# Key pages of a paged attention laid across partitions in quarters, queries block-diagonal

## The reference

```
x = x + 1/2 * SwiGLU_1(RMSNorm(x))
z = RMSNorm(x) @ w_in         # pooling u, attention q k v (6 heads x 64), retention q k v g
x = x + concat(pooling, attention, retention) @ w_out
x = x + 1/2 * SwiGLU_2(RMSNorm(x))
```

```
gate[block] = mean over the block's keys of q.k     # 4 past blocks of 256 keys
3 of the 4 past blocks are kept, the one with the lowest gate is dropped
s[key] = q.k / 8 - slope[h] * (position of q - position of key)
p = softmax(s over kept past keys and own keys up to j);   out = p @ v
```

## Time and profile before

| | |
|---|---|
| median of 3 runs | 1308.75 us |
| the profiled execution | 1308.36 us, span 1306.7 us, 1.66 us around it |
| TensorE, matmul | busy 1296.9 us (99%), 10969 instructions |
| TensorE, weight loads | 1253.0 us (96%) |
| DVE | 764.6 us (59%) |
| ACT | 650.2 us (50%) |
| GpSimd | 232.7 us (18%) |
| granted TensorE clock, mean | 0.998 |
| DMA | 233.18 MB, mean 178 GB/s |

### The profile page before, as it was taken

How to read it: one execution, slowest core, us unless ns; L and a number is a source line. 1 busy time by engine, 2 the same in 40 slices (tenths; PEclk the granted TensorE clock), 3 DMA queues, 4 the chain that set the end, 5 groups by cost and what they waited for, 6 DMA issues and landing times.

```text
span 1306.7 us, 27046 instructions
## 1 busy us (share of the span) xinstructions
PE 1296.9 (99%) x10969; PEld 1253.0 (96%) x10969; DVE 764.6 (59%) x787; ACT 650.2 (50%) x734; POOL 232.7 (18%) x372
## 2 busy tenths in 40 slices
PE   9999999999999999999999999999999999999998
PEld 7999999999879999999999999999998799999998
DVE  5555555677676655644555555565866675555433
ACT  6555543435463655553365555333446456555433
POOL 1020000357541000000101000012865220000010
PEclk9999999999999999999999999999999999999999
DMA  6665444658895444444445554446589844444442
GB/s 196 201 211 185 161 139 151 208 177 227 262 350 170 133 161 145 144 153 145 153 156 183 183 174 132 149 149 215 168 254 321 284 129 161 160 133 157 145 149 68
DMA packets 211423, 233.18 MB, mean 178 GB/s; under 512 B 14974, under 2 KB 205192, under 8 KB 211348
## 3 DMA queue, kind: packets, MB, share of 16 engines
q1 hardware_dynamic: 203388, 209.10, 50.1%
q0 software_dynamic: 7840, 23.01, 5.3%
q10 hardware_dynamic: 120, 0.03, 0.0%
HBM read 226.90 MB, written 5.32 MB: 178 GB/s over the span
## 4 chain that ended last, share of the span: by engine, by line
PE 96%; DMA 1%; DVE 1%; SPq 1%; issue 0%; ACT 0%; ACTq 0%; DVEq 0%
PE ps L1427 24%; PE ps L1429 24%; PE ps L1428 24%; PE ps L1547 4%; PE ps L1549 4%; PE ps L1548 4%; PE ps L1698 2%; PE ps L1736 2%; DMA kbuf<-in_cache_k 1%; PE ps L1875 1%; PE ps L1877 1%; PE ps L1876 1%; PE ps L1716 1%; PE ps L1588 1%; SPq L403 0%; DMA g_rows<-in_pool_scale 0%
## 5 line engine op out<-in xcount | busy, mean ns | idle before, releaser
L695 ACT ACTIVATE w_hi<-w_raw 128x2048 fp32r<-128x2048 f32 x167 | 319.8, 1915 | 521.6 <-PE ps L1429 418.5
L1007 DVE TENSOR_TENSOR w_lo<-w_raw,w_hi 128x2048 fp32r<-128x2048 f32 x159 | 366.1, 2303 | 194.4 <-ACT w_hi L695 190.0
L1427 PE MATMUL ps<-h_hi,w_hi 128*128 128x320 f32 x768 | 237.9, 310 | 0.7 <-DVE h_lo L1093 0.7
L1429 PE MATMUL ps<-h_hi,w_lo 128*128 128x320 f32 x768 | 237.3, 309 | 0.0
L1428 PE MATMUL ps<-h_lo,w_hi 128*128 128x320 f32 x768 | 237.3, 309 | 0.0
L1427 PE MATMUL ps<-g_hi,w_hi 128*128 128x320 f32 x704 | 218.0, 310 | 0.0
L1429 PE MATMUL ps<-g_hi,w_lo 128*128 128x320 f32 x704 | 217.5, 309 | 0.0
L1428 PE MATMUL ps<-g_lo,w_hi 128*128 128x320 f32 x704 | 217.5, 309 | 0.0
L1427 PE MATMUL ps<-act_hi,w_hi 128*128 128x320 f32 x704 | 216.5, 308 | 0.0
L1428 PE MATMUL ps<-act_lo,w_hi 128*128 128x320 f32 x704 | 216.5, 308 | 0.0
L1429 PE MATMUL ps<-act_hi,w_lo 128*128 128x320 f32 x704 | 216.5, 308 | 0.0
(11 more groups left out here) (295 smaller groups left out, 1734.0 us busy)
## 6 DMA issues: line engine op xcount, KB each, us to landing
w_raw<-in_ffn_w_in SPq DMA_DIRECT2D x87, 1024.0 KB, 5.1
w_raw<-in_ffn_w_out SPq DMA_DIRECT2D x32, 896.0 KB, 4.8
w_raw<-in_w_in SPq DMA_DIRECT2D x22, 1024.0 KB, 5.5
kbuf<-in_cache_k SPq DMA_DIRECT2D x96, 192.0 KB, 3.2
w_raw<-in_ffn_w_out SPq DMA_DIRECT2D x16, 1024.0 KB, 5.2
w_raw<-in_w_out SPq DMA_DIRECT2D x8, 1024.0 KB, 7.1
kbuf<-in_cache_k POOLq DMA_DIRECT2D x32, 192.0 KB, 3.0
kbuf<-in_cache_v SPq DMA_DIRECT2D x32, 192.0 KB, 4.3
```

Of the source, the lines that this page charges most:

```text
L695: act.activation(w_hi[:, slot, :], w_raw[:, slot, :], ACT.Copy).then_inc(hi_done, 1)
L1007: dve.tensor_tensor(w_lo[:, slot, :], w_raw[:, slot, :], w_hi[:, slot, :].bitcast(F32), ALU.subtract).then_inc(split_done, 1)
L1427: pe.matmul(out, w_hi[:, slot, w], hi[:, k, :], start=(k == 0), stop=False)
L1429: ins = pe.matmul(out, w_lo[:, slot, w], hi[:, k, :], start=False, stop=(k == k_all - 1))
```

## The change

The key pages of a sequence are loaded four side by side: page 4*half + j goes to partitions 32j to 32j+31, four consecutive tokens (6144 bytes) on one partition. After the same DVE transposes, partitions 32a to 32a+31 hold the dimensions of page a of a group of four. The queries are laid block-diagonally: on partitions 32a to 32a+31 only columns 8a to 8a+7 are filled. A product then uses all 128 rows and 32 columns; output row (sequence, head half g, page a, query), and the three heads of g lie side by side in columns: 768 past scores and 3 x 32 own scores a row, in banks 2 and 3. A row no longer holds all keys of a query, so that block sums, maxima and sums of exponentials are brought together by 32x32 transposes on DVE. Copies that reorder the transposed probabilities are more and smaller, and the three addr_align calls go away (the table is empty).

```
-                        sp_e.dma_start(kbuf[home][:, 4 * half + j, :],
-                                       A["cache_k"][L, page[j]].rearrange("t h d -> t (h d)")).then_inc(k_landed[home][half], 16)
+                        sp_e.dma_start(kbuf[home][32 * j:32 * j + 32, 4 * half:4 * half + 4, :],
+                                       A["cache_k"][L, page[j]].rearrange("(t r) h d -> t r (h d)", r=4)).then_inc(k_landed[home][half], 16)
```

```
 def qprep(L, p):
-                for bb in range(2):
-                    for gg in range(2):
-                        ...
-                        ins = pool.tensor_copy(dst.rearrange("p s (j c) -> p s j c", j=2)[:, :, :, 0:8],
-                                               q_rep[:, 3 * gg:3 * gg + 3, :, p * 16 + 8 * bb:p * 16 + 8 * bb + 8])
+                for a in range(4):
+                    r = slice(32 * a, 32 * a + 32)
+                    for bb in range(2):
+                        dst = q_sc[p][r, 384 * bb:384 * bb + 384].rearrange("p (x c) -> p x c", c=32)[:, :, 8 * a:8 * a + 8]
+                        src = q_rep[r, :, :, p * 16 + 8 * bb:p * 16 + 8 * bb + 8].rearrange("p h j q -> p (h j) q")
+                        ins = pool.tensor_copy(dst, src)
...
```

```
 def exps(p, parts=range(9)):
+                        n, part = divmod(k, 3)
+                        a, b = (256 * n + P * part, 256 * n + P * part + P) if part < 2 else (768 + 32 * n, 800 + 32 * n)
+                        at_b = 32 * part + n
+                        ins = act.activation(sp[p][:, a:b], sp[p][:, a:b], ACT.Exp, bias=bias_s[:, at_b:at_b + 1],
+                                             accum_out=blk[:, at_b:at_b + 1])
 def probs_evac(p):
+                    for n in range(3):
+                        ...
+                        for quad in range(2):
+                            at = 256 * (n % 2) + P * quad
+                            past = ps[:, t_bank(p, n // 2), at:at + P].rearrange("p (g a q) -> p g a q", g=4, a=4)
+                            to = pt[:, 384 * quad:384 * quad + 384].rearrange("p (a g n q) -> p g a n q", a=4, g=4, n=3)[:, :, :, n, :]
+                            ins = act.activation(to, past, ACT.Copy)
+                        ...
+                    for bb in range(2):
+                        ...
+                        act.activation(to, own, ACT.Copy)
-                exps(3, (0, 1))
+                exps(3, range(4))
                 out_evac(0)
                 act.wait_ge(stored_va, 16 * (L + 1))
                 att_evac(2)
-                exps(3, (2, 3, 4))
+                exps(3, range(4, 9))
```

```
 def soft_in(p):
+                    raw = ps[:, 2:4, :].rearrange("p b n -> p (b n)")
+                    dve.tensor_reduce(past_blocks(0), raw[:, 0:768].rearrange("p (n k x) -> p n k x", n=3, k=2), AX, ALU.add)
+                    dve.tensor_tensor(sp[p][:, 0:768].rearrange("p (k t r) -> p k r t", k=6, r=4), raw[:, 0:768]..., cst["alibi_s"][:]..., ALU.add)
+                    dve.tensor_tensor(sp[p][:, 768:864], raw[:, 768:864], cst["alibi_own"][:, p, :], ALU.add).then_inc(sm_in, 1)
+                    dve.drain()
+                    dve.tensor_reduce(past_blocks(2), sp[p][:, 0:768].rearrange("p (n k x) -> p n k x", n=3, k=2), AX, ALU.max)
+                    dve.tensor_reduce(blk[:, 128:131], sp[p][:, 768:864].rearrange("p (n x) -> p n x", n=3), AX, ALU.max)
 def soft_bias(p):      # a drain stands between steps that depend on each other
+                    dve.transpose(blk[:], blk[:])                          # 128 x 160
+                    dve.tensor_tensor(w, sums..., sums..., ALU.add)        # 128 x 32
+                    dve.tensor_tensor(peak..., peaks..., peaks..., ALU.max)
+                    dve.tensor_reduce(peak[:, 4, :], blk[:, 128:160]..., AX, ALU.max)
+                    dve.tensor_reduce(least, w..., AX, ALU.min)
+                    dve.tensor_tensor(w, w, each(least, 4), ALU.is_le)
+                    dve.tensor_tensor(w, w, cst["rank"]..., ALU.mult)
+                    dve.tensor_reduce(last, w..., AX, ALU.max)
+                    dve.tensor_tensor(w, w, each(last, 4), ALU.is_equal)
+                    dve.scalar_tensor_tensor(out=peak..., in0=w, scalar=-BIG, in1=peak..., op0=ALU.mult, op1=ALU.add)
+                    dve.tensor_reduce(top, peak..., AX, ALU.max)
+                    for e in range(2): dve.scalar_tensor_tensor(out=bias_s..., in0=w, scalar=-BIG, in1=each(top, 4), ...)
+                    dve.tensor_scalar(bias_s[:, 64:96]..., each(top, 4), -1.0, None, ALU.mult)
+                    dve.transpose(bias_s[:], bias_s[:]).then_inc(sm_bias, 1)   # 128 x 96
 def soft_sum(p):       # transpose 96, reduce, multiply by own_head, transpose 32, reduce, reciprocal: 6 for 2
```

```
-                FETCH = {2: 99, 5: 0, 10: 244}
+                FETCH = {}
+                def key_scores(p):
+                    pe.wait_ge(kt_ok, L * 16 + p * 4 + 4)
+                    for n in range(3):
+                        for j in range(2):
+                            for g in range(4):
+                                c = (3 * (g % 2) + n) * HD + 32 * j
+                                at_q = 192 * g + 64 * n + 32 * j
+                                ins = pe.matmul(ps[32 * g:32 * g + 32, 2 + n // 2, 256 * (n % 2):256 * (n % 2) + 256],
+                                                q_sc[p][:, at_q:at_q + 32], kbuf[k_home(p, g // 2)][:, :, c:c + 32],
+                                                start=(j == 0), stop=(j == 1))
```

More of the change, by code:

```diff
@@ L545, in qprep @@
                     r = slice(HD * half, HD * half + HD)
-                    own = q_bd[r, 0:192].rearrange("p (b x) -> p b x", b=2)
-                    for f in range(3):
-                        ins = pool.tensor_copy(own[:, :, 8 * half + 40 * f:8 * half + 40 * f + 8],
-                                               q_smp[r, f, p * 16:p * 16 + 16].rearrange("p (b q) -> p b q", b=2))
+                    own = q_bd[r, :].rearrange("p (f x) -> p f x", f=3)[:, :, 40 * half:40 * half + 40]
+                    for bb in range(2):
+                        ins = pool.tensor_copy(own[:, :, 32 * bb:32 * bb + 8],
+                                               q_smp[r, :, p * 16 + 8 * bb:p * 16 + 8 * bb + 8])
                 ins.then_inc(qb_ok, 1)
@@ L845, in ret_square, with exps @@
                     act.activation(o_sq[:, f, :], ps[:, 6, 0:TOK], ACT.Square).then_inc(o_sqd, 1)
[L847 removed]
+                def exps(p, parts=range(9)):
                     if 0 in parts:
                         act.wait_ge(sm_bias, L * 4 + p + 1)
[L850 to L854 removed]
+                    for k in parts:
+                        n, part = divmod(k, 3)
[3 more added lines that the diff above has]
+                                             accum_out=blk[:, at_b:at_b + 1])
+                    if 8 in parts:
                         ins.then_inc(sm_exp, 1)
@@ L1215, in soft_bias @@
                     dve.drain()
-                    dve.tensor_scalar(ss[:, 32:37], ss[:, 20:25], ss[:, 30:31], None, ALU.subtract).then_inc(sm_bias, 1)
+                    dve.tensor_reduce(last, w.rearrange("p c q -> p q c"), AX, ALU.max)
+                    dve.drain()
+                    dve.tensor_tensor(w, w, each(last, 4), ALU.is_equal)
+                    dve.drain()
+                    dve.scalar_tensor_tensor(out=peak[:, 0:4, :], in0=w, scalar=-BIG, in1=peak[:, 0:4, :], op0=ALU.mult, op1=ALU.add)
@@ new lines, in soft_bias @@
+                    dve.drain()
+                    dve.tensor_reduce(top, peak.rearrange("p c q -> p q c"), AX, ALU.max)
+                    dve.drain()
+                    for e in range(2):
+                        dve.scalar_tensor_tensor(out=bias_s[:, 0:64].rearrange("p (c e q) -> p c e q", e=2, q=NT)[:, :, e, :],
+                                                 in0=w, scalar=-BIG, in1=each(top, 4), op0=ALU.mult, op1=ALU.subtract)
+                    dve.tensor_scalar(bias_s[:, 64:96].rearrange("p (a q) -> p a q", q=NT), each(top, 4), -1.0, None, ALU.mult)
@@ new lines, in soft_sum @@
+                    dve.drain()
+                    dve.tensor_tensor(ss[:, 0:32].rearrange("p (n q) -> p n q", q=NT), ss[:, 32:40].unsqueeze(1).to_broadcast([P, 4, NT]),
+                                      cst["own_head"][:].unsqueeze(2).to_broadcast([P, 4, NT]), ALU.mult)
+                    dve.drain()
+                    dve.transpose(ss[:, 0:32], ss[:, 0:32])
+                    dve.drain()
+                    dve.tensor_reduce(ss[:, 96:97], ss[:, 0:3], AX, ALU.add)
+                    dve.drain()
@@ L1714, in transpose_probs @@
                         pe.wait_ge(pt2_evac, L * 8 + p * 2)
-                    for j in range(8):
+                    for j in range(6):
                         ins = pe.transpose(ps[:, t_bank(p, j // 4), P * (j % 4):P * (j % 4) + P], sp[p][:, P * j:P * j + P], ident[:])
@@ L1718, in transpose_probs @@
                             ins.then_inc(pt2_done, 1)
```

(6 more changed lines are left out.)

138 lines of the change are left out of this document (67 added, 71 removed).

## The result

| | before | after |
|---|---|---|
| median of the runs | 1308.88 us (1308.27 to 1309.34) | 1320.05 us (1318.97 to 1325.3) |
| ratio of the times, 95% interval | | 1.0094 (1.0067 to 1.0121) |
| profiled execution, span | 1308.36, 1306.7 us | 1318.97, 1317.1 us |

The change makes the kernel 0.94% slower. Forecast was 1312.0 with a range of 1300 to 1319: slower is right, the size is not, and the time lies 1 us outside the range.

The account below looks back on a forecast made before the run. The prediction took TensorE, busy 99% of the span, as the bound. A layer's terms, -5.0 + 2.6 + 1.8 + 0.3 + 2.0 + 0.1 = +1.8, twice +3.6, on 1308.4 gave 1312.0 us; range 1300 to 1319.

Parts of the forecast that it names:

- the clock: A clock under 1.00 behind the new waits was named only as a sign; the sum leaves it out.
- TensorE's products: key_scores in 2.62 us for 3.95, a gain of 1.33; with own_scores -1.24 a pair, -5.0 us a layer.
- DVE's string: On DVE before evac_last of the same chunk: soft_in -0.65 and soft_bias +2.0, together +1.35 us.
- Wait 1: Scores of pair 1: TensorE comes earlier, DVE's maxima later, so it stands +2.6 us, bounds 0.5 and 3.6.
- Wait 2: Scores of pairs 2 and 3: key pages written to 32 partitions land later, +1.8 us a layer.
- Rival B: At pairs 2 and 3 the key pages land in time, the sum without 1.8: 1308.4 us; chance 0.22.
- rival D: Half-rate key pages decide at pairs 2 and 3, +11.6 us in all: 1320.0 us; chance 0.11.
- Wait 3: Chunk boundaries around soft_bias(1) to (3), evac_last waiting behind DVE's longer string: +0.3 us a layer, 0 to 1.5.
- Wait 4: Pooling products L1842, fed by a longer chain from chunk 11's end to vr_tokens: +2.0 us a layer, 0 to 3.
- Instruction offsets: The three offset calls only shift TensorE's instruction stream: 0, bounds -1 and +2.5 us in all.
- C: TensorE's gain survives, decided on DVE between soft_in(0) and smax(1): 1298.5 to 1303.5 us; chance 0.20.

Follow-up runs that it names:

- e4_scores_only: Kernel before with only key_scores changed, to 24 products of 128 rows: 1300.19 us, ratio 0.9936.
- e6_scores_bias: Kernel before with key_scores changed to 24 products and soft_bias longer by 9 dependent DVE operations, key loads as before: 1315.87 us.
- f3_short_bias: Changed kernel without six dependent steps of soft_bias, so that no block is dropped: 1310.23 us, ratio 1.0019.
- e1_no_smax: Changed kernel without TensorE's three waits for the prompt's maxima before the scores of pairs 1, 2 and 3: 1321.08 us.
- e3_filler: Changed kernel with 21 extra TensorE products in front of the wait for the maxima at pair 1: 1322.50 us.
- e7_quarter_loads: Kernel before with each key page loaded onto 32 partitions, four tokens in a row: 1312.84 us, ratio 1.0032.
- e2_old_loads: Changed kernel with each key page loaded over all 128 partitions, as before: 1315.54 us.
- e8_no_fetch: Kernel before with the table of offsets empty and nothing else: 1318.39 us, ratio 1.0075.
- g6_row_write: g5_ordered with the bias added in output order, DVE reading PSUM with a stride and writing in a row: 1316.24 us.
- f2_fine_lo: e1_no_smax with GpSimd's lo_split in 16 operations of 128 columns in place of 4 of 512: 1316.39 us, ratio 1.0065.
- g5_ordered: f2_fine_lo with the o_past copies ahead of turn_k(3,0), and out_evac(0) and two vr_tokens earlier on ACT: 1317.42 us.
- g2_best: f2_fine_lo with TensorE reading the keys with a stride, o_past ahead of turn_k(3,0) and ACT reordered; computes something else: 1336.02 us.
- f1_v_order: Changed kernel with value pages loaded in the order of the scores and the bias added without its stride: 1440.05 us.

## Why the prediction was wrong in size

Two terms failed, and they belong together: DVE's longer string was sized +1.35 us and measured +2.3 and +3.0, and the clock that falls in the wait it causes was put at nothing and cost 3.9 us.

- **TensorE's products: right.** 2.62 us forecast, 2.62 measured; 8 x 1.33 = 10.6 us less the 2.4 waited at pair 1 is 8.2, and e4_scores_only gained 8.7.
- **DVE's string: the step that failed, by size.** I scaled soft_in by columns ("three passes over 768: -0.9") and forecast 3.2 us. It took 287.03 - 283.28 = 3.75, because the bias is now written with a stride of 4: 1.54 us for 0.94. soft_bias took 3.88 for 3.6, and 4.63 at the same place of the second layer. Together +2.3 and +3.0 for +1.35. A part of this was in my own items: 11 steps of 0.27, four of 0.1 to 0.2 and two transposes of 0.2 to 0.3 add up to 3.8 to 4.4 us, not 3.6.
- **Wait 1 and the clock: right mechanism, too small, and a term put at nothing.** 3.35 and 3.89 us for 2.6. The sum also left out the clock, which I named only as a sign: 1.4 and 2.5 us of the scores at 1.2 GHz. It is the largest single error of the sum. Waits (0.75 + 1.29) and clock (3.9) are 5.9 us of the 6.8 by which the span grew more than the 3.6 forecast.
- **What a microsecond of DVE costs.** I charged DVE's growth once a layer, at pair 1, and 0.3 for all else. e6_scores_bias charges 15.7 us for 23.4 us more of soft_bias, f3_short_bias gives back 9.8 for 14.6 less: about 0.67 us a microsecond both times. TensorE's starts say where. Held against e4_scores_only, e6_scores_bias loses 7.5 us up to pair 1, 4.1 from there to pair 2 (3.9 of them the scores at the lower clock), 1.7 to pair 3 and 3.3 to the pooling products, both layers together. So pair 1 was the tight place that I read in the earlier trace rows (13.96 of 14.80 us busy), and the end of the part the second; between pairs 2 and 3 DVE had some slack. What I missed is that a wait at pair 1 costs its own length and the clock on top. e1_no_smax and e3_filler add that what is saved there stays saved in the first layer (2.9 and 1.9 us) and is lost in the second (4.6 and 5.1 us), where DVE's operations on q_dec then meet GpSimd's lo_split.
- **Wait 2: right.** +1.8 a layer forecast; e7_quarter_loads gives 3.7 for both layers, e2_old_loads 4.5. The pages land 0.9 us apart (e7_quarter_loads: their first parts at 305.10, 306.02 and 306.89 us) where they were 0.5 to 0.7 apart. Rival B falls, and D's end is reached in the total but not by D's cause. The Trainium skill, page "SBUF — State Buffer", section "Door 1: The DMA port swizzle", says that partitions 0 to 31 reach 8 of the 16 ports, as 0 to 63 do. The landings agree in direction; the price, about 2 us a layer, was a third of the 6.1 us that its full effect gave in rival D.
- **Wait 3: wrong place.** 0.3 a layer forecast at the moves; 1.5 us in two waits stood before pair 3, where TensorE waits for the prompt's probabilities that ACT makes behind exps(2) and probs_evac(0).
- **Wait 4: right in the sum.** 2.0 forecast; 1.5 + 0.7 and 1.2 + 0.7 measured. Only the 0.7 stands at L1896, for vr_tokens; the larger part stands before it, for out_evac(0), which ACT does amid the exponentials of exps(3).
- **Instruction offsets: right for the changed kernel, wrong as reasoned.** I bounded them by +2.5 because no wait for instructions stood in the list. The list was clean because the table worked: without it the kernel before is 9.1 us slower. The changed kernel was spared, since its key_scores has a quarter of the instructions or lies elsewhere in the stream; which of the two, no run decides. That my term of 0 held is in this sense luck.
- **A rival's sum.** C's -5.0 + 0.5 + 0 is -4.5 a layer and not -5.0, so its lower end is 1299.4. It plays no part in the outcome.

What stays open: what the fine lo_split alone does to the changed kernel (it ran only together with e1_no_smax), whether a new table would help the changed kernel, and what soft_sum, the exponentials and the copies cost; none of these was run alone.

## What to carry to other kernels

When a faster step on the busiest engine lengthens the small dependent work of a second engine, price the wait where that engine has no lead together with the clock that falls in it, and then look for the next place behind it: about 0.67 us were lost here for each microsecond added to DVE. If an experiment puts in a stand-in for such work, measure the stand-in: nine operations meant as 2.3 us took 2.9 on average. Scale a tensor operation by its columns only if its access order stays the same; a stride in what it writes made 0.94 into 1.54 us. And a clean list of waits does not show that a tuning device is useless; it may be clean because of it.

## What the runs showed of the hardware

- Near the end of an idle time of TensorE of 3.35 us (waiting for an engine), and 1.4 us behind one of 2.89 us (no engine waited for, e8_no_fetch), the granted clock fell to 0.50 for 3.4 us; in the second layer, in 3.89 us of idle time, for 6.8 us. In g6_row_write it fell in 2.65 us of idle time, for 3.4 us. In f2_fine_lo and g5_ordered, whose longest wait is 1.9 us, it stayed at 1.00 to the end of the work.
- DVE's multiplications into q_dec (both inputs in SBUF) are held up by GpSimd's lo_split, which reads SBUF: six took 1.00 us alone, 4.84 beside operations of 1.26 us, 2.57 beside operations a quarter as wide. The Trainium skill, page "SBUF — State Buffer", section "Who interferes with whom", says that a DVE instruction with two inputs in SBUF contends with a GpSimd instruction that reads SBUF; these rows agree.
- 48 instructions of float32 products of 128 rows took 6.38 us with moving columns 1536 bytes apart (g2_best), and 2.80 with runs of 32 columns side by side.
- A DVE addition over 768 columns took 1.54 us with its output written at a stride of 4 elements, 0.94 us with the output in a row (f1_v_order), and 0.94 us with a stride of 32 columns on the PSUM operand (g6_row_write).
- A value page loaded as four interleaved groups of rows took SyncE about 3 us to issue in a row of twelve, for 0.67; the DMA share was 0.27 and the rate 93 GB/s meanwhile (f1_v_order).
- Key pages of 192 KB loaded onto 32 partitions each landed 0.9 us apart, for 0.5 to 0.7 on 128 (e7_quarter_loads).
